# A fourth Strassen step per gate and up chunk, with part of the weight sums formed by accumulating transfers

## The chip, the cores and the metric

The kernel runs on one core of one Trainium2 chip. The metric is the device time of one execution in microseconds (us). Engines are named as in the profile: PE is TensorE's matmul, PEld its weight load, DVE is VectorE, ACT is ScalarE, POOL is GpSimd, SP is SyncE, which here only starts transfers.

## The reference

Two transformer blocks in float32 on 256 tokens of width 2048. The change touches only the gate and up products of the second block's feed-forward part (width 5632, that is 11 chunks of 512 columns):

```
h2 = rms_norm(x, g_ffn[i])
x = x + (jax.nn.silu(h2 @ w_gate[i]) * (h2 @ w_up[i])) @ w_down[i]
```

## The kernel before

**Products.** Every matrix product is done three times over: an operand is split into `hi` (rounded to the float32r type) and `lo` (what is left), and a product is hi x hi + lo x hi + hi x lo. The weights are what moves: they come from memory in items of 1 MB (128 partitions, 4 pieces or "quads" of 512 columns), ACT writes `whi` (a rounding copy, L1673), DVE writes `wlo` (raw minus whi, L2288), and PE consumes both. Every item is one unit of the order of work, and each engine takes the items in the same order. `whi` and `wlo` have three slots (SPLIT), so the conversion of item g can begin when PE has finished item g-3 (`mm_done`). The raw tile has a ring of four slots in this stage; SP starts the next load into a slot when DVE has finished with it.

**Pairs.** A chunk of gate and up takes the 16 blocks of 128 rows of h2 in 8 pairs. A pair of token tiles x a pair of row blocks times (gate, up) is a 2 x 2 by 2 x 2 block product. It is done either directly (kind D: 8 block products, 24 matmuls of 512 columns, one item) or by Strassen's scheme (kind S: 7 block products, 21 matmuls), and `GUD_PLAN` says which: before, "DDSDSDSD". A pair of kind S is two items. The first, B, uses three of the raw quads as they are (9 matmuls). The second, T, uses four sums of quads (12 matmuls), built from the same load: with u0, u1 the two up quads and g0, g1 the two gate quads, the sums are u0+u1, g1+u1, then the second plus u0, and that plus g0. DVE forms the first two in one instruction of 1024 columns (L2296), the third in L2299, the fourth in L2301; ACT rounds them in two halves (L1680), and DVE subtracts in two halves (L2305).

**Chunk end.** At the end of a chunk DVE folds the PSUM banks of the products (L2777, L2780, L2787, L2790), ACT applies silu (L2226), DVE multiplies (L3050); the hidden tile is transposed by PE (L1330) ahead of steps 4 and 6 of the next chunk and split by ACT and DVE (L1721, L2335). These instructions stand at fixed places between the conversions of the items, which ACT and DVE make two items ahead of PE's place in the chunk. Chunks come in blocks of 4, 4 and 3; behind each block the down projection runs with plain items (24 matmuls each, L857 to L862).

**First chunk.** In the first of the 11 chunks the last two pairs of h2's own tiles are still being built by ACT and DVE between the items (`gud_f`, `gud_hi`, `gud_lo`).

Of the kernel before, what the change touches and what calls it, by code (L numbers as in the profile page):

```python
# [25 lines left out]
F32 = mybir.dt.float32  # L26
# [7 lines left out]
P = 128  # L34
# [158 lines left out]

FF1_PLAN, FF2_PLAN, GUD_PLAN = "DDSDDSDD", "DDSDDSDD", "DDSDSDSD"
FF_BLOCKS, GUD_PAIRS = 4, (4, 4, 3)
# [50 lines left out]
ITEM_OF = [g for g in range(len(KINDS)) if KINDS[g] != "T"]  # L246
SLOTS = 5


# [54 lines left out]
def build(nc, a, out):  # L304
# [3 lines left out]
    with ctx:  # L308
# [73 lines left out]
        ff2_t = tiles("ff2", FF2_PLAN, W_AT, W_AT + tile_bytes(FF2_PLAN))  # L382
        gud_t = tiles("gud", GUD_PLAN, B_AT, W_AT + 16 * KB)
        E_AT = A_AT + 2 * tile_bytes(FF1_PLAN)
# [75 lines left out]
        def sem(name):  # L460
            return ctx.enter_context(nc.semaphore(name))
# [35 lines left out]
        fill_free, gate_b0 = sem("fill_free"), sem("gate_b0")  # L497
        mm_half, w_hi_half = sem("mm_half"), sem("w_hi_half")
        t_sum, t_hi, f_in, f_sum = sem("t_sum"), sem("t_hi"), sem("f_in"), sem("f_sum")
        bank_done, s1_out, q_free, silu_done, gud_hid = map(sem, (  # L500
# [144 lines left out]
        def v2(ap):  # L645

            return ap.rearrange("p (t n) -> p t n", t=2)
# [3 lines left out]
        def _(sp):  # L651
# [22 lines left out]
            def load_pair(src1, src2, c, step):  # L674

                n = w.n["group"]
                room(n)
                into = raw_of(n).rearrange("p (k f n) -> p k f n", k=2, f=2)
                for f, src in enumerate((src1, src2)):
                    sp.dma_start(into[:, :, f, :], src[:, 2 * step:2 * step + 2, c:c + COLS]  # L680
                                 ).then_inc(raw_in[SLOT[n]], 16)
                w.n["group"] += 1
# [108 lines left out]
        def _(pool):  # L791
            with nc.allow_non_contiguous_dma(reason="small rows"):
# [27 lines left out]
                for n, g in enumerate(("q_norm_2", "k_norm_2")):  # L820
                    pool.dma_start(qkg[:, n, :], a[g].rearrange("(a n) -> a n", a=1).to_broadcast([P, D2])
                                   ).then_inc(con2_in, 16)

                pool.wait_ge(w_lo, MARK["gud_end"])
                pool.wait_ge(mm_done, MARK["gud_end"])
# [829 lines left out]
        def _(act):  # L1655
# [19 lines left out]
            def sums_hi(g):  # L1675

                for n in range(2):
                    act.wait_ge(t_sum, 2 * SUMS_BEFORE[g] + 1 + n)
                    part = slice(2 * n * COLS, 2 * (n + 1) * COLS)
                    nc.scalar.activation(whi[:, g % SPLIT, part], tsum[:, g % SPLIT, part], ACT.Copy  # L1680
                                         ).then_inc(w_hi if n else t_hi, 1)

# [581 lines left out]
        def _(dve):  # L2264
# [26 lines left out]
            def weight_sums(g):  # L2291

                slot, r, n = g % SPLIT, raw_of(load_of(g)), SUMS_BEFORE[g]
                t = tsum[:, slot, :]
                dve.wait_ge(mm_done, g + 1 - SPLIT)
                V.tensor_tensor(v2(t[:, 0:2 * COLS]), both(r[:, col(3)]), v2(r[:, COLS:3 * COLS]), ALU.add  # L2296
                                ).then_inc(t_sum, 1)
                dve.wait_ge(t_sum, 2 * n + 1)
                link(V.tensor_tensor(t[:, col(2)], t[:, col(1)], r[:, col(1)], ALU.add))  # L2299
                linked()  # L2300
                V.tensor_tensor(t[:, col(3)], t[:, col(2)], r[:, col(0)], ALU.add).then_inc(t_sum, 1)  # L2301
                for k in range(2):
                    dve.wait_ge(w_hi if k else t_hi, g + 1 if k else n + 1)
                    part = slice(2 * k * COLS, 2 * (k + 1) * COLS)
                    last = V.tensor_tensor(wlo[:, slot, part], t[:, part], whi[:, slot, part].bitcast(F32),  # L2305
                                           ALU.subtract)
                last.then_inc(w_lo, 1)
# [843 lines left out]
```

## Time and profile before

| | |
|---|---|
| median of 3 runs | 2763.66 us (2761.6 to 2764.61) |
| profiled execution | 2762.97 us, its span 2761.2 us |
| PE busy | 2736.2 us, 99% |
| DVE busy | 1882.3 us, 68% |
| ACT busy | 1406.1 us, 51% |
| POOL busy | 14.8 us, 1% |
| DMA | 508.18 MB, mean 184 GB/s |

Shares over the whole span average stages of different kinds. The stage of the change runs from 1940 to 2589 us with the down projections in it, and what bounds it is read there. A row that gives an engine's idle time names what ended that idle time. The spans on POOL are those of issuing a transfer; how long the transfer itself took is given as the time from issue to landing.

### The profile page before, as it was taken

To read this page: it belongs to the slowest core of one execution; us is meant where nothing else is said; L and a number is where in the kernel's file an instruction comes from. 1 tells how busy PE (TensorE), PEld (TensorE's weight loads), DVE (VectorE), ACT (ScalarE), POOL (GpSimd) and SP (SyncE) were. 2 spreads that over 40 slices of the span, in tenths; PEclk is the share of its full clock that TensorE was granted. 3 is DMA by queue.
4 is the path that set the end of the run, shared out by engine and by line. 5 is a ranking of instruction groups with operands and counts; after the bars stand their busy time and mean duration, and the time that the engine had idled before them with its cause. 6 is when DMAs were issued, how large, how long until landed. Compare 5 with 4: busy or idle time off the path is not lost.

```text
span 2761.2 us, 30992 instructions
## 1 busy us (share of the span) xinstructions
PE 2736.2 (99%) x12990; PEld 2270.7 (82%) x12990; DVE 1882.3 (68%) x1699; ACT 1406.1 (51%) x1532; POOL 14.8 (1%) x28
## 2 busy tenths in 40 slices
PE   9999999999999999999999999999999999999999
PEld 7888778888888888888888888888788888888887
DVE  5445765455468878878788685665788488659765
ACT  5435663345556556465465544344554355435553
POOL 0000000000000000000000000000000000000000
PEclk9999999999999999999999999999999999999999
DMA  7745036555445555555555654545556555656555
GB/s 235 222 147 168 31 108 211 191 190 198 170 153 201 188 205 176 201 199 186 209 189 182 217 196 149 183 157 197 195 188 210 197 183 198 214 181 200 185 180 173
DMA packets 225082, 508.18 MB, mean 184 GB/s; under 512 B 9570, under 2 KB 20400, under 8 KB 224048
## 3 DMA queue, kind: packets, MB, share of 16 engines
q1 hardware_dynamic: 222752, 495.62, 53.6%
q0 software_dynamic: 2016, 10.36, 1.2%
q8 instruction: 103, 1.69, 0.2%
q14 instruction: 35, 0.29, 0.0%
q10 hardware_dynamic: 176, 0.23, 0.0%
HBM read 504.08 MB, written 2.10 MB: 183 GB/s over the span
## 4 chain that ended last, share of the span: by engine, by line
PE 79%; DVE 5%; ACT 2%; issue 1%; DMA 1%; ACTq 0%
PE acc L857 13%; PE acc L858 13%; PE acc L862 13%; PE acc L1340 6%; PE acc L1341 6%; PE acc L1345 6%; PE tb L1345 6%; PE tb L1340 6%; PE tb L1341 6%; DVE wlo L2288 2%; ACT whi L1673 1%; PE tb L842 1%; PE tb L1330 1%; DVE ff_lo L2757 1%; DVE tsum L2296 0%
## 5 line engine op out<-in xcount | busy, mean ns | idle before, releaser
L2288 DVE TENSOR_TENSOR wlo<-raw,whi 128x2048 fp32r<-128x2048 f32 (+2 forms) x465 | 1023.8, 2212 | 570.0 <-ACT whi L1673 569.3
L1673 ACT ACTIVATE whi<-raw 128x2048 fp32r<-128x2048 f32 (+2 forms) x465 | 858.0, 1853 | 593.1 <-PE acc L862 315.5
L857 PE MATMUL acc<-whi,ahi 128*128 128x512 f32 (+1 forms) x1456 | 566.6, 390 | 0.9 <-ACT z L1713 0.5
L858 PE MATMUL acc<-whi,alo 128*128 128x512 f32 (+1 forms) x1456 | 562.2, 387 | 0.0
L862 PE MATMUL acc<-wlo,ahi 128*128 128x512 f32 (+1 forms) x1456 | 357.6, 387 | 0.0
L857 PEld LDWEIGHTS acc<-whi,ahi 128*128 128x128 f32 x1456 | 273.9, 188 | 56.6 <-ACT z L1713 0.9
L858 PEld LDWEIGHTS acc<-whi,alo 128*128 128x128 f32 x1456 | 274.1, 188 | 54.4
L862 PEld LDWEIGHTS acc<-wlo,ahi 128*128 128x128 f32 x1456 | 271.0, 188 | 55.5
L1680 ACT ACTIVATE whi<-tsum 128x1024 fp32r<-128x1024 f32 x130 | 138.1, 1062 | 264.6 <-DVE tsum L2296 239.2
L1340 PE MATMUL acc<-whi,ff_hi 128*128 128x512 f32 x512 | 202.2, 395 | 7.2 <-DVE h L2360 3.9
L1341 PE MATMUL acc<-whi,ff_lo 128*128 128x512 f32 x512 | 199.8, 390 | 0.0
L1340 PE MATMUL tb<-whi,ff_hi 128*128 128x512 f32 x480 | 189.1, 394 | 0.0
L1341 PE MATMUL tb<-whi,ff_lo 128*128 128x512 f32 x480 | 187.3, 390 | 0.0
L1345 PE MATMUL acc<-wlo,ff_hi 128*128 128x512 f32 x512 | 163.2, 390 | 0.0
L2305 DVE TENSOR_TENSOR wlo<-tsum,whi 128x1024 fp32r<-128x1024 f32 x130 | 158.4, 1222 | 0.0
L1345 PE MATMUL tb<-wlo,ff_hi 128*128 128x512 f32 x480 | 156.2, 390 | 0.0
L1340 PE MATMUL acc<-whi,gud_hi 128*128 128x512 f32 x352 | 138.0, 392 | 3.2 <-ACT whi L1680 2.1
L1341 PE MATMUL acc<-whi,gud_lo 128*128 128x512 f32 x352 | 137.4, 390 | 0.0
L1340 PE MATMUL tb<-whi,gud_hi 128*128 128x512 f32 x319 | 125.8, 395 | 0.0
L1341 PE MATMUL tb<-whi,gud_lo 128*128 128x512 f32 x319 | 124.4, 390 | 0.0
L1340 PEld LDWEIGHTS acc<-whi,ff_hi 128*128 128x128 f32 x512 | 96.1, 188 | 29.3 <-DVE ff_lo L2757 4.4
L1345 PE MATMUL acc<-wlo,gud_hi 128*128 128x512 f32 x352 | 116.2, 391 | 0.0
(408 smaller groups left out, 3653.1 us busy)
## 6 DMA issues: line engine op xcount, KB each, us to landing
raw<-in_w_ff SPq DMA_DIRECT2D x128, 1024.0 KB, 5.0
raw<-in_w_in SPq DMA_DIRECT2D x119, 1024.0 KB, 5.1
raw<-in_w_gate SPq DMA_DIRECT2D x88, 512.0 KB, 3.9
raw<-in_w_up SPq DMA_DIRECT2D x88, 512.0 KB, 4.8
raw<-in_w_down SPq DMA_DIRECT2D x44, 1024.0 KB, 5.1
raw<-in_w_out SPq DMA_DIRECT2D x16, 1024.0 KB, 5.2
raw<-in_w_o SPq DMA_DIRECT2D x16, 1024.0 KB, 5.1
raw<-in_w_ple_gate SPq DMA_DIRECT2D x16, 1024.0 KB, 5.2
```

Source lines behind the costliest of these rows:

```text
L842: last = nc.tensor.transpose((into or tb[w.n["turn"] % 2])[:, n * P:(n + 1) * P], src, ident)
L857: nc.tensor.matmul(out_(t), hi[:, kt, tt(t)], whi[:, slot, wc(k)], start=first and k == 0, stop=False)
L858: nc.tensor.matmul(out_(t), lo[:, kt, tt(t)], whi[:, slot, wc(k)], start=False, stop=False)
L862: mm = nc.tensor.matmul(out_(t), hi[:, kt, tt(t)], wlo[:, slot, wc(k)], start=False, stop=last and k == len(kts) - 1)
L1330: last = nc.tensor.transpose(turn_bank[:, n * P:(n + 1) * P], src, ident)
L1340: nc.tensor.matmul(o, t.hi[:, tile, :], whi[:, slot, col(quad)], start=start, stop=False)
L1341: nc.tensor.matmul(o, t.lo[:, tile, :], whi[:, slot, col(quad)], start=False, stop=False)
L1345: return nc.tensor.matmul(o, t.hi[:, tile, :], wlo[:, slot, col(quad)], start=False, stop=stop)
L1673: nc.scalar.activation(whi[:, g % SPLIT, 0:n_], raw_of(n)[:, 0:n_], ACT.Copy).then_inc(w_hi, 1)
L1680: nc.scalar.activation(whi[:, g % SPLIT, part], tsum[:, g % SPLIT, part], ACT.Copy).then_inc(w_hi if n else t_hi, 1)
L2288: V.tensor_tensor(wlo[:, g % SPLIT, 0:n_], raw_of(load_of(g))[:, 0:n_], whi[:, g % SPLIT, 0:n_].bitcast(F32), ALU.subtract).then_inc(w_lo, 1)
L2305: last = V.tensor_tensor(wlo[:, slot, part], t[:, part], whi[:, slot, part].bitcast(F32), ALU.subtract)
```

## The change

`GUD_PLAN` becomes "DDSSDSSD": four pairs of kind S (steps 2, 3, 5, 6) and four of kind D. The first two of the four weight sums of every T item of this stage (u0+u1 and g1+u1) are no longer formed by DVE. POOL starts two plain transfers into a tile `tpre` (u0 and g1, 256 KB each), waits for both (`pre_in`), and starts two accumulating transfers that add u1 to each half (`pre_sum`). There are two such tiles, used in turn; the loads for the n-th sum wait until DVE has finished T item n-2 (`w_lo`). ACT rounds the first half and DVE subtracts it straight from `tpre`; DVE still forms the third and fourth sum. Since u1 as a raw quad is then used by nobody, SP leaves it out of the load of an S pair (768 KB instead of 1 MB). The feed-forward part of the first block has its own plans and keeps DVE's sums.

```diff
-FF1_PLAN, FF2_PLAN, GUD_PLAN = "DDSDDSDD", "DDSDDSDD", "DDSDSDSD"
+FF1_PLAN, FF2_PLAN, GUD_PLAN = "DDSDDSDD", "DDSDDSDD", "DDSSDSSD"
+SUM_ITEM = [g for g in range(len(KINDS)) if KINDS[g] == "T"]
+GUD_SUMS = SUMS_BEFORE[MARK["gud"]]
...
-        gud_t = tiles("gud", GUD_PLAN, B_AT, W_AT + 16 * KB)
+        gud_t = tiles("gud", GUD_PLAN, B_AT, W_AT + 12 * KB)
+        tpre = [sb("tpre0", [P, 2, COLS], F32, W_AT + 8 * KB), sb("tpre1", [P, 2, COLS], F32, B_AT + 27 * KB)]
...
                 for f, src in enumerate((src1, src2)):
-                    sp.dma_start(into[:, :, f, :], src[:, 2 * step:2 * step + 2, c:c + COLS]
+                    ks = 1 if f and GUD_PLAN[step] == "S" else 2
+                    sp.dma_start(into[:, 0:ks, f, :], src[:, 2 * step:2 * step + ks, c:c + COLS]
                                  ).then_inc(raw_in[SLOT[n]], 16)
...
+                pool.wait_ge(mm_done, MARK["gud"] - 3)
+                wg, wu, n = ktiles(a["w_gate_2"]), ktiles(a["w_up_2"]), 0
+                for b, pairs in enumerate(GUD_PAIRS):
+                    for c in range(pairs):
+                        for step in [k for k in range(len(GUD_PLAN)) if GUD_PLAN[k] == "S"]:
+                            at = slice((4 * b + c) * COLS, (4 * b + c + 1) * COLS)
+                            into = tpre[n % 2]
+                            if n >= 2:
+                                pool.wait_ge(w_lo, SUM_ITEM[GUD_SUMS + n - 2] + 1)
+                            pool.dma_start(into[:, 0, :], wu[:, 2 * step, at]).then_inc(pre_in, 16)
+                            pool.dma_start(into[:, 1, :], wg[:, 2 * step + 1, at]).then_inc(pre_in, 16)
+                            pool.wait_ge(pre_in, 32 * (n + 1))
+                            for k in range(2):
+                                pool.dma_start(into[:, k, :], wu[:, 2 * step + 1, at], accum_op=ALU.add
+                                               ).then_inc(pre_sum, 16)
+                            n += 1
...
+                m = SUMS_BEFORE[g] - GUD_SUMS
                 for n in range(2):
-                    act.wait_ge(t_sum, 2 * SUMS_BEFORE[g] + 1 + n)
                     part = slice(2 * n * COLS, 2 * (n + 1) * COLS)
-                    nc.scalar.activation(whi[:, g % SPLIT, part], tsum[:, g % SPLIT, part], ACT.Copy
-                                         ).then_inc(w_hi if n else t_hi, 1)
+                    src = tsum[:, g % SPLIT, part]
+                    if m >= 0 and n == 0:
+                        act.wait_ge(mm_done, g + 1 - SPLIT)
+                        act.wait_ge(pre_sum, 32 * (m + 1))
+                        src = tpre[m % 2][:, :, :].rearrange("p k n -> p (k n)")
+                    else:
+                        act.wait_ge(t_sum, 2 * SUMS_BEFORE[g] + 1 + n)
+                    nc.scalar.activation(whi[:, g % SPLIT, part], src, ACT.Copy).then_inc(w_hi if n else t_hi, 1)
...
+                m = n - GUD_SUMS
+                pre = t[:, 0:2 * COLS] if m < 0 else tpre[m % 2][:, :, :].rearrange("p k n -> p (k n)")
+                if m < 0:
...
+                else:
+                    dve.wait_ge(pre_sum, 32 * (m + 1))
+                    V.tensor_tensor(t[:, col(2)], pre[:, col(1)], r[:, col(1)], ALU.add).then_inc(t_sum, 1)
+                    dve.wait_ge(t_sum, 2 * n + 1)
                 V.tensor_tensor(t[:, col(3)], t[:, col(2)], r[:, col(0)], ALU.add).then_inc(t_sum, 1)
```

What the change does to the order of DVE's instructions, in the conversions of the items from the first B of a chunk on. In the names, `tsum` is the tile of sums, `tpre` the new tiles, numbers behind a name are those of the buffers. Before (one B and T, a D, the next B and T):

```order
L2288 TENSOR_TENSOR wlo<-raw_108,whi 128x1536 [waits w_hi]
L2296 TENSOR_TENSOR tsum<-raw_108 128x1024 [waits mm_done]
L2299 TENSOR_TENSOR tsum<-tsum,raw_108 128x512 [waits t_sum]
L2301 TENSOR_TENSOR tsum<-tsum,raw_108 128x512 [waits v_link]
L2305 TENSOR_TENSOR wlo<-tsum,whi 128x1024 [waits t_hi]
L2305 TENSOR_TENSOR wlo<-tsum,whi 128x1024 [waits w_hi]
L2288 TENSOR_TENSOR wlo<-raw_109,whi 128x2048 [waits w_hi]
L2288 TENSOR_TENSOR wlo<-raw,whi 128x1536 [waits w_hi]
L2296 TENSOR_TENSOR tsum<-raw 128x1024 [waits mm_done]
L2299 TENSOR_TENSOR tsum<-tsum,raw 128x512 [waits t_sum]
```

The same place now, where the lines have moved down in the file (L2288 is L2315, L2305 is L2338):

```order
L2315 TENSOR_TENSOR wlo<-raw_110,whi 128x1536 [waits w_hi]
L2332 TENSOR_TENSOR tsum<-tpre_103,raw_110 128x512 [waits pre_sum,mm_done]
L2334 TENSOR_TENSOR tsum<-tsum,raw_110 128x512 [waits t_sum]
L2338 TENSOR_TENSOR wlo<-tpre_103,whi 128x1024 [waits t_hi]
L2338 TENSOR_TENSOR wlo<-tsum,whi 128x1024 [waits w_hi]
L2315 TENSOR_TENSOR wlo<-raw_111,whi 128x1536 [waits w_hi]
L2332 TENSOR_TENSOR tsum<-tpre_104,raw_111 128x512 [waits pre_sum,mm_done]
L2334 TENSOR_TENSOR tsum<-tsum,raw_111 128x512 [waits t_sum]
L2338 TENSOR_TENSOR wlo<-tpre_104,whi 128x1024 [waits t_hi]
L2338 TENSOR_TENSOR wlo<-tsum,whi 128x1024 [waits w_hi]
L2315 TENSOR_TENSOR wlo<-raw,whi 128x2048 [waits w_hi]
L2315 TENSOR_TENSOR wlo<-raw,whi 128x1536 [waits w_hi]
```

The instruction of 1024 columns that began each T item is gone, its first instruction now waits for `pre_sum` as well, and two S pairs follow each other without a D item between them.

POOL's queue in this stage, where it had nothing before. L838 and L839 are the plain transfers, L842 the accumulating ones:

```order
L838 DMA tpre_103<-in_w_up 128x512 [waits w_lo]
L839 DMA tpre_103<-in_w_gate 128x512
L842 DMA tpre_103<-in_w_up 128x512 [waits pre_in]
L842 DMA tpre_103<-in_w_up 128x512
L838 DMA tpre_104<-in_w_up 128x512 [waits w_lo]
L839 DMA tpre_104<-in_w_gate 128x512
L842 DMA tpre_104<-in_w_up 128x512 [waits pre_in]
L842 DMA tpre_104<-in_w_up 128x512
```

POOL carries two waits per sum, one for the tile to be free and one for its own loads; the loads of one sum stand behind the accumulating transfers of the sum before it in the same queue.

## Rows read from the trace of the kernel before

**Rows 1.** The page's part 1, busy time.
```profile
PE 2736.2 (99%) x12990; PEld 2270.7 (82%) x12990; DVE 1882.3 (68%) x1699; ACT 1406.1 (51%) x1532; POOL 14.8 (1%) x28
```

**Rows 2.** Critical chain through the stage: start us, us, what.
```profile
1938.95 1.81 PE acc L862 x8
...
2051.54 0.91 PE tb L1345 x4
2093.99 0.91 PE tb L1345 x4
```

**Rows 3.** Windows: the first chunk, a later chunk, a PE gap, the stretch after it.
```profile
core 0: us, PE busy (x) PEld busy (x) DVE busy (x) ACT busy (x) POOL busy (x), PEclk, DMA share, GB/s
1940.00:1985.00 45.00, 41.76 (x179) 33.43 (x178) 33.93 (x34) 25.56 (x27) 0.00 (x0) 0.96 0.47 147
2009.09:2051.54 42.45, 42.45 (x192) 35.12 (x192) 37.88 (x32) 23.00 (x20) 0.00 (x0) 1.00 0.61 199
1976.70:1978.85 2.15, 0.04 (x2) 0.00 (x1) 2.12 (x4) 1.76 (x3) 0.00 (x0) 1.00 0.11 9
1980.40:1983.40 3.00, 3.00 (x9) 2.32 (x8) 2.77 (x2) 2.00 (x2) 0.00 (x0) 0.50 0.61 232
```

**Rows 4.** What PE waited for from 1935 to 2000 us: total, times, longest.
```profile
PE acc L1340 <- ACT whi L1680: 2.1, 1, 2.1
PE acc L1340 <- ACT whi L1673: 1.1, 1, 1.1
```

**Rows 5.** Groups in the later chunk, by shape: busy us, mean ns, idle before.
```profile
L2288 DVE TENSOR_TENSOR wlo<-raw,whi 128x2048 fp32r<-128x2048 f32 x5 | 11.4, 2289 | 3.8 <-ACT whi L1673 3.8
L2305 DVE TENSOR_TENSOR wlo<-tsum,whi 128x1024 fp32r<-128x1024 f32 x7 | 8.5, 1222 | 0.0
L2288 DVE TENSOR_TENSOR wlo<-raw,whi 128x1536 fp32r<-128x1536 f32 x3 | 5.3, 1753 | 0.0
L2296 DVE TENSOR_TENSOR tsum<-raw 128x1024 f32<-128x1024 f32 x3 | 3.7, 1219 | 0.0
L2301 DVE TENSOR_TENSOR tsum<-tsum,raw 128x512 f32<-128x512 f32 x3 | 2.1, 692 | 0.1
L1680 ACT ACTIVATE whi<-tsum 128x1024 fp32r<-128x1024 f32 x7 | 7.4, 1063 | 12.4 <-DVE tsum L2296 10.8 <-DVE tsum L2301 1.6
```

**Rows 6.** DVE's timeline in the first chunk, ahead of PE's 2.1 us wait.
```profile
1975.04 1.22 DVE L2296 TENSOR_TENSOR tsum<-raw 128x1024 f32<-128x1024 f32 x1
...
1977.01 0.69 DVE L2301 TENSOR_TENSOR tsum<-tsum,raw 128x512 f32<-128x512 f32 x1
```

**Rows 7.** A later chunk: PE's first matmul, DVE's end of its first T item.
```profile
2073.66 0.39 PE L1340 MATMUL acc<-whi,gud_hi 128*128 128x512 f32 x1
2082.69 2.43 DVE L2305 TENSOR_TENSOR wlo<-tsum,whi 128x1024 fp32r<-128x1024 f32 x2
```

**Rows 8.** Transfers in the later chunk; columns of part 2 in 40 slices.
```profile
GB/s 83 313 409 197 2 0 29 179 405 351 50 195 403 355 8 0 27 172 401 405 388 332 230 120 345 401 158 0 0 8 58 311 409 210 0 0 68 309 409 203
raw<-in_w_up SPq DMA_DIRECT2D x9, 512.0 KB, 4.8
raw<-in_w_gate SPq DMA_DIRECT2D x8, 512.0 KB, 3.9
```

**Rows 9.** Transfers of POOL's queue: KB each, us from issue to landing.
```profile
gfin<-in_g_final POOLq DMA_DIRECT2D x1, 1024.0 KB, 5.2
bple<-in_b_ple_gate POOLq DMA_DIRECT2D x1, 1024.0 KB, 4.9
pin<-in_p POOLq DMA_DIRECT2D x1, 256.0 KB, 6.0
grows<-in_g_ffn POOLq DMA_DIRECT2D x1, 8.0 KB, 2.8
```

**Rows 10.** POOL's timeline at the end of the stage, the issues of two of these.
```profile
2588.52 0.54 POOL L826 DMA_DIRECT2D bple<-in_b_ple_gate  x1 [1047.85 <-PE tb L1345]
2589.05 0.71 POOL L828 DMA_DIRECT2D pin<-in_p  x1
```

More of the change, by code:

```diff
@@ L498, in build @@
         mm_half, w_hi_half = sem("mm_half"), sem("w_hi_half")
+        pre_in, pre_sum = sem("pre_in"), sem("pre_sum")
         t_sum, t_hi, f_in, f_sum = sem("t_sum"), sem("t_hi"), sem("f_in"), sem("f_sum")
@@ L2295, in weight_sums @@
                 dve.wait_ge(mm_done, g + 1 - SPLIT)
[L2296 to L2300, printed above, removed]
+                m = n - GUD_SUMS
+                pre = t[:, 0:2 * COLS] if m < 0 else tpre[m % 2][:, :, :].rearrange("p k n -> p (k n)")
+                if m < 0:
+                    V.tensor_tensor(v2(pre), both(r[:, col(3)]), v2(r[:, COLS:3 * COLS]), ALU.add).then_inc(t_sum, 1)
+                    dve.wait_ge(t_sum, 2 * n + 1)
+                    link(V.tensor_tensor(t[:, col(2)], pre[:, col(1)], r[:, col(1)], ALU.add))
+                    linked()
+                else:
+                    dve.wait_ge(pre_sum, 32 * (m + 1))
+                    V.tensor_tensor(t[:, col(2)], pre[:, col(1)], r[:, col(1)], ALU.add).then_inc(t_sum, 1)
+                    dve.wait_ge(t_sum, 2 * n + 1)
                 V.tensor_tensor(t[:, col(3)], t[:, col(2)], r[:, col(0)], ALU.add).then_inc(t_sum, 1)
@@ L2304, in weight_sums @@
                     part = slice(2 * k * COLS, 2 * (k + 1) * COLS)
-                    last = V.tensor_tensor(wlo[:, slot, part], t[:, part], whi[:, slot, part].bitcast(F32),
-                                           ALU.subtract)
+                    last = V.tensor_tensor(wlo[:, slot, part], t[:, part] if k else pre,
+                                           whi[:, slot, part].bitcast(F32), ALU.subtract)
                 last.then_inc(w_lo, 1)
```

## The prediction

> **What bounds the kernel now.** I read the page's first part, then the chain through the stage, then windows inside it, the groups of one chunk, the waits, and last the transfers. PE is busy 99% of the span [rows 1], so only fewer or faster matmuls make the kernel faster, unless a new wait appears. In the stage of the change the chain is PE's: eight matmuls of 512 columns take 1.81 us, 0.227 us each, and a chunk follows the other in 42.45 us [rows 2]. Three S pairs (21 matmuls each) and five D pairs (24 each) are 183 matmuls, 41.5 us; the two sets of transposes take the other 0.97 us. In that chunk PE has no idle time at all, while DVE works 37.9 of the 42.45 us and ACT 23.0 [rows 3]. So DVE is the engine that is near: its 89% can't be raised by much.
>
> **PE.** A fourth S pair in place of a D pair takes 3 matmuls out of each chunk: 3 x 0.227 = 0.68 us, in 11 chunks 7.5 us. That is all that the change can give in the steady chunks.
>
> **DVE.** Per T item the add of 1024 columns (1.22 us) goes, and one of 512 (0.69 us) now reads the finished sum; the rest is unchanged: 0.69 + 0.69 + 2 x 1.22 = 3.8 us instead of 5.0 [rows 5]. Per chunk: three T items save 3.7 us; the D pair that becomes an S pair gives up 2.3 us and takes 1.75 + 3.8 [rows 5]. The balance is -3.7 + 3.3 = -0.4 us, so about 37.5 of 41.8 us. ACT gets the B and T copies (1.5 + 2 x 1.06 us [rows 5]) for one of 1.9 us, with 18 us free. Neither becomes the bound by its sum. What matters is the order: the pairs of kind S now touch. I lay the chunk out from PE's first matmul, with 5.44 us per D, 2.04 per B, 2.72 per T item and 0.49 ahead of steps 4 and 6. PE's items then end at 5.4, 10.9, 12.9, 15.6, 17.7, 20.4, 26.3, 28.4, 31.1, 33.6, 36.3 and 41.8 us. An item's conversion starts when PE is done with the third item before it. The last B may start at 26.3: ACT 1.5, DVE 1.75, so DVE turns to the last T at 29.6, adds twice until 31.0, ACT's second half is done at 32.1, and PE wants it at 33.6: it is hidden by 1.5 us. DVE's subtractions end at 33.5, the split of the transposed tile at 34.1, and the last D's `wlo` (ACT's copy from 32.7 to 34.6, then 2.3 us) at 36.9, where PE asks for it after two matmuls at 36.8. That is a wait of 0.1 to 0.2 us that is new; I take 0.17 in the 8 chunks that have such transposes, 1.4 us. If DVE were faster nothing more would come, if it were slower by some tenths each would be paid 11 times.
>
> **The accumulating transfers** are the part whose price the trace does not show. The path that decides is the last sum of a chunk. Its tile and that of the sum before it come free when DVE ends T items 2 and 1. Before, DVE ends the first T 11.5 us after PE's first matmul (2085.1 against 2073.7 [rows 7]); with 1.22 us less work, and the rest of the schedule as above, 10.7 is what I take. From there POOL has until 29.6 us, when DVE turns to the last T: 18.9 us. In them it must, one behind the other, load sum 3's tile, accumulate into it, load sum 4's tile (behind those accumulations in the same queue), and accumulate into that. POOL's second wait, for its own loads, is what makes this serial; behind the waiting instruction stand the next sum's loads, and ACT and DVE both wait for `pre_sum` in front of all later conversions, so PE is next. With F for the fixed part of a transfer from issue to landing, L for moving a pair of loads (512 KB) and A for a pair of accumulations, the path is 3F + 2L + 2A (one F is shared, since the loads of sum 4 follow sum 3's accumulations in the queue).
> F: POOL's 1 MB transfers land 4.9 and 5.2 us after issue [rows 9]; at the 409 GB/s that the slices of the later chunk reach [rows 8] the moving is 2.6 us of it, so 2.3 to 2.6 us are fixed; 8 KB take 2.8. I take 2.5. SP's pairs agree: the second of two 512 KB loads, issued some 0.4 us behind the first, lands after 4.8 [rows 8].
> L: alone 0.52 MB at 409 GB/s is 1.3 us. The high end is the transfer of 256 KB that was issued at 2589.05 and landed 6.0 us later, 1.6 us behind the one issued at 2588.52 that took 4.9 [rows 9, 10]: twice that is 3.3 us. SP's loads run in bursts with free slices between them [rows 8], so I take 1.8, nearer to the low end.
> A: the low end is a plain load alone, 1.3 us. An accumulation has to read its destination as well as its source; the high end is twice the slow row, 6.6 us. I take 3.3, the slow row itself, because that is the nearest POOL transfer beside SP's.
> Path: 7.5 + 3.6 + 6.6 = 17.7 us, hidden by 1.2 us. At the low ends it is 6.9 + 2.6 + 2.6 = 12.1, hidden by 7; at the high ends 8.4 + 6.6 + 13.2 = 28.2, late by 9.3 in every chunk. The point from which it binds is L + A = 5.7 us. The other three sums of a chunk have more room, since a D or the chunk's turn lies before them.
> The Trainium skill ("Collectives: The Full Stack", Part 3, the section on the bandwidth ceiling) has a rule that speaks against the change: a reducing transfer has two source reads and so moves at half the rate of a copy. By it A would be 2.6 us alone and about 3.6 beside SP's loads, and the path 16.3 to 18.3 us: still hidden, but by little. No row of this trace shows an accumulation, so the rule is neither borne out nor refuted here.
>
> **The transfers as a whole.** A chunk moved 8 x 1.05 = 8.4 MB at a DMA share of 0.61 [rows 3]. Now SP moves 7.3 MB, POOL 2.1 MB plain and 2.1 MB accumulating. Plain bytes alone are a share of about 0.70; the accumulations add 0.15 if they cost as much as plain ones and 0.31 at twice that. There is room, but little at the upper price, and SP's loads, issued some 10 us ahead, would be the first to use it up.
>
> **The first chunk.** There DVE is late: PE is idle 3.24 of 45.0 us [rows 3], 2.1 and 1.1 us of it waiting for ACT's copies [rows 4]. The larger wait hangs on a T item, whose sums run from 1975.04 to 1977.7, then ACT's copy [rows 6]. Behind that gap the granted clock is 0.50 for 3.0 us [rows 3], that is 1.2 instead of 2.4 GHz; in these 3.0 us PE does the work of 1.5, so the gap costs 1.5 us more. With 1.2 us less in every T item, and T items one D earlier, the two waits shrink: I put the remainder at 1.2 us and the gap too short for the clock to fall, which would give 3.5 us, and take 2.5, between a full recovery (4.7) and a loss of 1.5 if the S pair that comes earlier lands on the building of the tiles.
>
> **The sum.** -7.5 + 1.4 - 2.5 = -8.6 us. From the profiled execution's 2762.97 us that is 2754.4; the median of the runs is 0.7 us above that execution, so 2755.
>
> **Rivals.**
> (B) The accumulating transfers take the place of DVE as the bound. At F 2.5, L 2.5 and A 4.4 the path is 21.3 us, late by 2.4 in each chunk. A chunk then takes 42.45 - 0.56 + 2.4 = 44.3, 11 of them cost 20 us, less 2.5 in the first: 2781. From a gap of about 2.1 us on, as in the first chunk, the clock can fall behind it, 1.5 us more each: 2797. For it: POOL's transfers of 256 KB land late beside SP's, and the path is serial. Against it: the bursts of rows 8 leave free slices, and the chain is short of binding by the prices taken.
> (C) Accumulations are far slower than copies (the high ends): late by 9.3 us, with the clock 10.2 net per chunk, 11 x 10.2 less 2.5: 2873. For it nothing but the absence of a row; against it that a copy's price would have to rise fivefold.
> (D) The sums are in time, but the denser order or the crowded transfers cost some tenths per item (SP's loads late, DVE's last D later than 0.17 us), or the first chunk gives nothing: 0.5 us more per chunk, 2760.
>
> **How the numbers follow.** The forecast (A) has 0.45, B 0.28, C 0.12, D 0.15. What a measurement of this kernel can tell from no change is about 0.2%, 5.5 us: below 2758.1 is faster, above 2769.2 slower. Faster: 0.38 of A, 0.04 of B (a lateness of some tenths), 0.02 of D: 0.44. Same: 0.07 of A, 0.04 of B, 0.09 of D: 0.20. Slower: 0.20 of B, 0.12 of C, 0.04 of D: 0.36. The forecast's own range is 2750 to 2760. The range for 8 in 10 goes up through B with the clock to 2803 and leaves C out.
>
> **What would show it.** Right: PE items of the stage without idle, a chunk period of 41.8 to 42.0 us, 33 matmuls fewer; POOL's accumulations landing within some 6 us of their issue; the first chunk's PE gaps under 1.5 us and the clock at 1.00. Wrong: PE or ACT waiting for a DMA into `tpre` in the last S pair of each chunk (B: 1 to 4 us, with a clock of 0.5 behind the longer ones; C: about 10 us), or ACT waiting for raw loads there (D). The forecast falls if L + A is above 5.7 us.

## The result and the profile after

The changed kernel takes 2807.59 us (median of 4 runs, 2803.14 to 2810.25) against 2764.14 us before, on the same chip: a ratio of 1.0156, 95% interval 1.0144 to 1.0168. It is slower by 43 us; the forecast was 9 us faster, and the time lies 4.6 us above the upper end of the range. The profiled execution took 2803.14 us, its span is 2801.3 us.

The page's part 1, which answers to [rows 1]:

```profile
PE 2744.8 (98%) x12957; PEld 2271.2 (81%) x12957; DVE 1877.5 (67%) x1713; ACT 1421.6 (51%) x1554; POOL 142.2 (5%) x204
```

The 33 matmuls are gone, yet PE is busy 8.6 us longer: some of the others ran at the lower clock. What PE waited for from 1935 to 2640 us (total, times, longest):

```profile
PE acc L1361 <- ACT whi L1708: 28.7, 12, 3.8
PE acc L1366 <- DVE wlo L2315: 4.1, 4, 1.1
PE acc L1361 <- ACT whi L1694: 1.8, 1, 1.8
```

L1708 is ACT's copy of a T item. Before, PE had 3.2 us of waits in the stage, all in the first chunk [rows 4]; now it has 34.6. That is 31.4 us more, and with 8.6 us more of busy time it makes the 40.1 us between the two spans to 0.1. Counted from one chunk's first fold on DVE to the next's inside a block, a chunk follows the other in 45.6 to 47.9 us (before 42.45, and 42.8 to 43.0 for the second chunk of a block).

The critical chain through one steady chunk (start us, us, what) says where the wait comes from:

```profile
2050.87 2.37 DVE wlo L2338 x2
2053.23 0.29 issue
2053.52 0.56 POOL tpre L838
2054.08 5.88 DMA tpre<-in_w_gate
2059.96 0.49 issue
2060.45 0.56 POOL tpre L842
2061.01 7.34 DMA tpre<-in_w_up
2068.44 0.70 DVE tsum L2332
2069.16 0.70 DVE tsum L2334
2069.89 1.07 ACT whi L1708
2071.00 0.49 PE acc L1361
2071.49 0.23 PE acc L1362
2071.73 0.23 PE tb L1361
2071.96 0.37 PE tb L1362
2072.33 0.43 PE acc L1361
```

DVE ends a T item and frees its tile at 2053.2, the last sum's two loads follow, then its accumulations, and 15.2 us later DVE can begin the last T item of the chunk. Before, the chain in the later chunks was PE's [rows 2]. DVE's timeline shows how long it stood there, and PE's what it cost (in brackets the idle time before, and what ended it):

```profile
2063.23 1.76 DVE L2315 TENSOR_TENSOR wlo<-raw,whi 128x1536 fp32r<-128x1536 f32 x1 [1.19 <-ACT whi L1694]
2068.44 0.69 DVE L2332 TENSOR_TENSOR tsum<-tpre,raw 128x512 f32<-128x512 f32 x1 [3.45 <-DMA tpre<-in_w_up]
```

```profile
2071.00 0.49 PE L1361 MATMUL acc<-whi,gud_hi 128*128 128x512 f32 x1 [2.10 <-ACT whi L1708]
```

The sum is late by 3.45 us for DVE; 1.3 us of it is hidden by the slack that the prediction counted (1.5 us), and PE stands for 2.1. Behind the gap some eight matmuls start 0.43 instead of 0.23 us apart, 1.6 us more in all. Windows (columns as in [rows 3]) of the two transfers of the path, of that slow stretch, and of a whole chunk:

```profile
2054.08:2060.45 6.37, 6.37 (x32) 5.26 (x31) 6.33 (x6) 3.45 (x4) 0.56 (x3) 1.00 1.04 346
2061.57:2068.35 6.78, 6.78 (x34) 5.60 (x33) 2.23 (x2) 1.49 (x1) 1.80 (x3) 1.00 1.01 274
2071.00:2075.30 4.30, 4.30 (x12) 3.40 (x13) 3.84 (x3) 4.03 (x3) 1.81 (x3) 0.60 1.00 237
2009.09:2055.00 45.91, 42.21 (x189) 34.25 (x188) 37.13 (x33) 24.31 (x21) 11.58 (x16) 1.00 0.87 252
```

Over a chunk the DMA engines are busy 0.87 of the time. In just the two stretches that the path passes through they are full (1.04 and 1.01; a share is the time of the packets that start in the window, so it can pass 1), and the second of them moves only 274 GB/s, against the 409 of plain loads [rows 8]. From issue to landing (KB each, median us) POOL's transfers take, from 1990 to 2600 us:

```profile
tpre<-in_w_up POOLq DMA_DIRECT2D x111, 256.0 KB, 6.6
tpre<-in_w_gate POOLq DMA_DIRECT2D x37, 256.0 KB, 5.7
```

SP fills the engines there. Its timeline over the same stretch:

```profile
2050.90 0.37 SPq L685 DMA_DIRECT2D raw<-in_w_gate  x1
2051.31 0.54 SPq L685 DMA_DIRECT2D raw<-in_w_up  x1
2056.12 0.37 SPq L685 DMA_DIRECT2D raw<-in_w_gate  x1
2056.53 0.47 SPq L685 DMA_DIRECT2D raw<-in_w_up  x1
2059.71 0.37 SPq L685 DMA_DIRECT2D raw<-in_w_gate  x1
2060.12 0.47 SPq L685 DMA_DIRECT2D raw<-in_w_up  x1
```

Three item loads start within 9 us. This is not chance: an item that DVE finishes frees a raw slot for SP and, if it is a T item, 2.4 us later a tile for POOL (DVE's fourth sum ends at 2050.87, its last subtraction at 2053.2).

### The profile page after: what moved, and what is told of

Same layout as the page of the kernel before. It is cut to its first block, busy times and chain, and to the rows that moved or that the text cites. A ratio compares the mean times of both kernels' runs of the same rounds, so it can differ in the third digit from the quotient of the medians.

```text
span 2801.3 us, 31226 instructions
## 1 busy us (share of the span) xinstructions
PE 2744.8 (98%) x12957; PEld 2271.2 (81%) x12957; DVE 1877.5 (67%) x1713; ACT 1421.6 (51%) x1554; POOL 142.2 (5%) x204
## 4 chain that ended last, share of the span: by engine, by line
PE 71%; DVE 7%; DMA 5%; ACT 4%; issue 2%; POOL 0%; ACTq 0%; DVEq 0%
PE acc L878 13%; PE acc L879 13%; PE acc L883 13%; PE acc L1361 5%; PE acc L1366 5%; PE acc L1362 5%; PE tb L1361 5%; PE tb L1362 5%; PE tb L1366 5%; DMA tpre<-in_w_up 3%; DVE wlo L2315 3%; ACT whi L1694 2%; DMA tpre<-in_w_gate 2%; DVE wlo L2338 1%; PE tb L863 1%
## 5 line engine op out<-in xcount | busy, mean ns | idle before, releaser
L2315 DVE TENSOR_TENSOR wlo<-raw,whi 128x2048 fp32r<-128x2048 f32 (+2 forms) x465 | 1018.8, 2200 | 577.1 <-ACT whi L1694 576.1
L1708 ACT ACTIVATE whi<-tsum 128x1024 fp32r<-128x1024 f32 x108 | 114.7, 1062 | 179.9 <-DVE tsum L2326 118.6
L2338 DVE TENSOR_TENSOR wlo<-tsum,whi 128x1024 fp32r<-128x1024 f32 x108 | 131.8, 1223 | 0.0
L1366 PE MATMUL acc<-wlo,gud_hi 128*128 128x512 f32 x352 | 122.0, 397 | 4.1 <-DVE wlo L2315 4.1
```

Of the source, the lines that this page charges most:

```text
L1366: return nc.tensor.matmul(o, t.hi[:, tile, :], wlo[:, slot, col(quad)], start=False, stop=stop)
L1708: nc.scalar.activation(whi[:, g % SPLIT, part], src, ACT.Copy).then_inc(w_hi if n else t_hi, 1)
L2315: V.tensor_tensor(wlo[:, g % SPLIT, 0:n_], raw_of(load_of(g))[:, 0:n_], whi[:, g % SPLIT, 0:n_].bitcast(F32), ALU.subtract).then_inc(w_lo, 1)
L2338: last = V.tensor_tensor(wlo[:, slot, part], t[:, part] if k else pre, whi[:, slot, part].bitcast(F32), ALU.subtract)
```

## The experiments

The theory (S) after reading this: two tiles make the last sum's load wait for the T item two before it, and load plus accumulation, beside SP's bursts, take longer than is left. Rivals: the denser order makes DVE late by itself (O); the bytes and accumulations load the DMA engines so that everything is late (T); the issues on POOL are the price (I). The expectations below call T "theory B"; it is not the prediction's rival B, which is S. Times before in these runs were 2764.06 to 2764.38 us.

**The plan alone.** The new plan, all sums formed by DVE, no transfers of POOL.

```diff
-GUD_SUMS = SUMS_BEFORE[MARK["gud"]]
+GUD_SUMS = 10 ** 6
...
-                    ks = 1 if f and GUD_PLAN[step] == "S" else 2
+                    ks = 2
...
-                pool.wait_ge(mm_done, MARK["gud"] - 3)
                 wg, wu, n = ktiles(a["w_gate_2"]), ktiles(a["w_up_2"]), 0
-                for b, pairs in enumerate(GUD_PAIRS):
+                for b, pairs in enumerate(()):
```

> One part of the change alone: the plan DDSSDSSD, with all four sums formed by DVE as before and u1 loaded by SP; POOL starts nothing. Theory S (the change is slow because the load-then-accumulate path of POOL is late for the last sums of a chunk, each late sum stopping PE): without transfers no wait on them, but DVE now has 42.4 us of work per chunk of 41.8, so DVE itself is late by some tenths to 2 us per chunk: 2762 to 2785 us. Theory O (the order with two S pairs side by side is what costs): as slow as the change or slower, 2800 us or more, with PE waiting for ACT's copy of the sums in the second pair of each group. Theory B (the DMA engines are full, raw loads are late): as S, since the bytes are those of before.

Measured: 2791.49 us, ratio 1.0099 [1.0084, 1.0114], 6.5 us above the range of theory S. A chunk takes 44.8 us; DVE works 42.1 of them and waits only for ACT's copies in between, so DVE sets the pace. What PE waited for in the stage, its two largest:

```profile
PE acc L1360 <- ACT whi L1707: 15.2, 23, 3.0
PE acc L1365 <- DVE wlo L2314: 11.1, 11, 1.2
```

So the fourth S pair needs the relief of DVE, and the changed kernel pays more for the relief than the plan costs without it.

**The transfers alone.** The old plan, its three sums per chunk formed by transfers.

```diff
-FF1_PLAN, FF2_PLAN, GUD_PLAN = "DDSDDSDD", "DDSDDSDD", "DDSSDSSD"
+FF1_PLAN, FF2_PLAN, GUD_PLAN = "DDSDDSDD", "DDSDDSDD", "DDSDSDSD"
```

> The other part alone: the plan of before (DDSDSDSD, three sums per chunk) with the first two sums formed by accumulating transfers. Theory S: the three sums stand a D pair apart and every tile is free 20 us or more ahead, so all are in time; PE's matmuls are those of before: 2761 to 2766 us. Theory B: 10.5 MB per chunk instead of 8.4 keep the DMA engines above 80%, raw loads or sums come late, 2770 us or more. Theory O: as before, 2764.

Measured: 2760.84 us, ratio 0.9987 [0.9977, 0.9996], chunks of 42.45 us as before, at a DMA share of 0.84 and 251 GB/s. That is nearly the share of the changed kernel (0.87), and nothing is late in steady chunks. A high mean share is not the cause by itself. Nearly all of the 3.5 us comes from the first chunk, which is 3.1 us shorter than before: PE waits 1.5 us there instead of 3.2, and the granted clock stays at 1.00. That is the relief of DVE which the prediction had counted on, still in the old order.

**A copy for the accumulation.** The same transfers, plain: the sum isn't formed.

```diff
-                                pool.dma_start(into[:, k, :], wu[:, 2 * step + 1, at], accum_op=ALU.add
+                                pool.dma_start(into[:, k, :], wu[:, 2 * step + 1, at]
```

> The changed kernel with the two accumulating transfers of each sum replaced by plain ones of the same size to the same place (so the sums hold u1 alone and the output is not the reference's). All waits and issues stay. Theory S with a dear accumulation (A is well above a copy's time): the second phase gets shorter by 1.5 to 3 us per sum, twice in the path, 2765 to 2785 us. If an accumulation costs what a copy costs and only the two serial phases matter: 2800 to 2808, no change. Theory B (full engines): between these, as far as the DMA share falls.

Measured: 2773.54 us, ratio 1.0032 [1.0021, 1.0043]. A transfer of the second pair lands 4.3 us after its issue instead of 6.9 (medians), an issue takes 0.54 instead of 0.90 us, and the gate load ahead of it lands after 4.6 us instead of 5.7. 34 of the 47 us above the free-running variants go; even with copies 13 remain.

**Nobody waits for the sums.** POOL forms the first two sums of the stage only, and all later T items use what is in the tiles.

```diff
                             if n >= 2:
+                                break
...
-                        act.wait_ge(pre_sum, 32 * (m + 1))
+                        act.wait_ge(pre_sum, 32 * min(m + 1, 2))
...
-                    dve.wait_ge(pre_sum, 32 * (m + 1))
+                    dve.wait_ge(pre_sum, 32 * min(m + 1, 2))
```

> The changed kernel with transfers into the two tiles for the first two sums only; all later sums use what lies there (so the output is not the reference's), nobody waits for POOL any more, and SP still leaves u1 out. It prices everything but the transfers. Theories S and B: the gain I forecast for the hidden case, 2753 to 2758 us, with chunk periods of 41.8 to 42.0 us. Theory O: 2775 us or more.

Measured: 2760.87 us, ratio 0.9989 [0.9979, 0.9998]. This is what the new order gives once the sums cost nothing: chunks of 42.08 us, 47 us less than the changed kernel, and still only 3.5 us less than before. So O is wrong as a cause of the loss, but the forecast of 2755 was out of reach even with sums for nothing.

**Three tiles.** A third tile (in two halves of 2 KB per partition), so that a sum's loads wait for the T item three before it; same transfers and same bytes, nothing is left out.

```diff
+        tpre2 = [sb("tpre2a", [P, COLS], F32, B_AT + 30 * KB), sb("tpre2b", [P, COLS], F32, W_AT + 38 * KB)]
+        pre_half = lambda m, k: tpre2[k][:, :] if m % 3 == 2 else tpre[m % 3][:, k, :]
...
-                            if n >= 2:
-                                pool.wait_ge(w_lo, SUM_ITEM[GUD_SUMS + n - 2] + 1)
-                            pool.dma_start(into[:, 0, :], wu[:, 2 * step, at]).then_inc(pre_in, 16)
+                            if n >= 3:
+                                pool.wait_ge(w_lo, SUM_ITEM[GUD_SUMS + n - 3] + 1)
+                            pool.dma_start(pre_half(n, 0), wu[:, 2 * step, at]).then_inc(pre_in, 16)
...
```

> The changed kernel with a third tile for the sums that are formed ahead, so that the loads of sum n wait for T item n-3 instead of n-2; bytes, accumulations and POOL's two-phase order stay (one tile in three is in two parts, which costs ACT 0.1 and DVE 0.2 us there). Theory S (each late sum is the two-phase path measured from the freeing of a tile): POOL then needs only 4 x (6.3 us for the loads + 1.8 for issuing the accumulations + some tenths) = 34 us per chunk of 42, the sums are in time and PE's waits on them go: 2761 to 2768 us. Theory B (the 16 DMA engines have no time left: a share of 0.87 over chunks of 45.8 us is 39.9 us, 0.95 of a chunk of 42): transfers get slower as the chunk gets shorter, and half or more of the loss stays: 2780 to 2805 us.

Measured: 2760.49 us, ratio 0.9987 [0.9977, 0.9997]. All 47 us are back. What PE waited for in the stage, and a window over a steady chunk:

```profile
PE acc L1364 <- ACT whi L1697: 1.8, 1, 1.8
PE acc L1364 <- ACT whi L1714: 1.8, 1, 1.8
```

```profile
2009.00:2051.00 42.00, 41.99 (x190) 34.37 (x189) 37.17 (x33) 24.45 (x23) 11.49 (x17) 1.00 0.90 271
```

The transfers are no faster (accumulations land after 6.5 us, loads after 6.3 to 6.8), the DMA share is higher (0.90), and PE has no idle time in the chunk. T is wrong: the same amount at a higher share costs nothing once the last sum may start earlier. Span by span it is 42.2 us: 31.0 of waits in the stage and 12.1 of PE's busy time (2732.7 against 2744.8), less 0.9 us by which PE's idle time outside the stage differs.

**The S pairs apart.** Two tiles, with D items between the first three S pairs.

```diff
-FF1_PLAN, FF2_PLAN, GUD_PLAN = "DDSDDSDD", "DDSDDSDD", "DDSSDSSD"
+FF1_PLAN, FF2_PLAN, GUD_PLAN = "DDSDDSDD", "DDSDDSDD", "DSDSDSSD"
```

> The changed kernel with the plan DSDSDSSD: the same four S pairs, 33 matmuls fewer, two tiles, the same transfers, but only one pair of S pairs side by side. Theory S: fewer T items have their tile freed less than 20 us ahead, and the sums arrive more evenly: 2765 to 2785 us. Theory B: the bytes are the same in the same time, so 2795 us or more. Should the first D item alone ahead of an S pair collide with DVE's folds at the chunk's start, PE waits for ACT's copy there, and the gain is lost with POOL in time.

Measured: 2786.7 us, ratio 1.0082 [1.0067, 1.0097]; waits for `whi` of T items 14.6 us in 11, for `wlo` of D items 8.8 in 9. 21 of the 47 us go, somewhat less than theory S had set (at most 2785). One pair of neighbours is left in the chunk, and its second sum still has too little time.

**One phase, plain.** Only the two loads, no accumulation: the tiles hold u0 and g1. POOL starts the loads of a sum when those of the sum before have landed.

```diff
+                            if n:
+                                pool.wait_ge(pre_in, 32 * n)
...
-                            pool.wait_ge(pre_in, 32 * (n + 1))
-                            for k in range(2):
-                                pool.dma_start(into[:, k, :], wu[:, 2 * step + 1, at], accum_op=ALU.add
-                                               ).then_inc(pre_sum, 16)
...
-                        act.wait_ge(pre_sum, 32 * (m + 1))
+                        act.wait_ge(pre_in, 32 * (m + 1))
...
-                    dve.wait_ge(pre_sum, 32 * (m + 1))
+                    dve.wait_ge(pre_in, 32 * (m + 1))
```

> The changed kernel with the accumulating transfers left out: ACT and DVE take the tiles as the two plain loads leave them (so the output is not the reference's). Each sum has one phase of some 5 us from the freeing of its tile, and 9.4 MB per chunk move. Theories S and B alike: in time, 2760 to 2763 us, as in the run with two sums only (2760.9). If it is slower than 2766, SP's raw loads are held up already by plain traffic.

Measured: 2761.51 us, ratio 0.9991 [0.9982, 1.0]; the loads land after 3.0 us.

**One phase, accumulating.** Only the two accumulations, onto what is in the tile (it is loaded once).

```diff
-                            pool.dma_start(into[:, 0, :], wu[:, 2 * step, at]).then_inc(pre_in, 16)
-                            pool.dma_start(into[:, 1, :], wg[:, 2 * step + 1, at]).then_inc(pre_in, 16)
-                            pool.wait_ge(pre_in, 32 * (n + 1))
+                                pool.wait_ge(pre_sum, 32 * n)
+                            if n < 2:
+                                for k, w_ in enumerate((wu[:, 2 * step, at], wg[:, 2 * step + 1, at])):
+                                    pool.dma_start(into[:, k, :], w_).then_inc(pre_in, 16)
+                            pool.wait_ge(pre_in, 32 * min(n + 1, 2))
```

> The changed kernel with only the accumulating transfers (after the first two sums no plain loads go ahead of them, so the tiles keep adding u1 and the output is not the reference's); POOL starts those of a sum when those of the sum before have landed. One phase again, now the dear one, of 6 to 8 us. Theory S: the last sum of a chunk has 11.6 us from the freeing of its tile, so it is in time: 2760 to 2765 us. If an accumulation hurts by what it takes from the DMA engines and not by its place in a two-phase path (theory B), a good part of the 47 us stays: 2775 us or more.

Measured: 2760.73 us, ratio 0.9988 [0.9978, 0.9997]; the accumulations land after 5.3 us. Together with the experiment in which nobody waits for the sums, these two price an accumulated byte. The same window in each, first without transfers of POOL, then with 2.1 MB plain, then with 2.1 MB accumulating:

```profile
2009.00:2051.00 42.00, 41.99 (x190) 34.41 (x189) 37.16 (x33) 24.41 (x22) 0.00 (x0) 1.00 0.56 176
```

```profile
2009.00:2051.00 42.00, 41.99 (x190) 34.41 (x189) 37.16 (x32) 24.39 (x22) 4.27 (x8) 1.00 0.69 226
```

```profile
2009.00:2051.00 42.00, 41.99 (x189) 34.44 (x188) 37.16 (x33) 24.41 (x22) 6.98 (x8) 1.00 0.85 226
```

The plain transfers add 0.13 to the DMA share, the accumulating ones 0.29 at the same 226 GB/s: 2.2 times the engine time for the same bytes. (The page's part 3 gives the same over the whole execution: POOL's queue has 1.5% of the engines' time with 12.46 MB, 3.8% with 33.44 MB and 6.8% with 34.49 MB, so 5.3% for 22.0 MB accumulated against 2.3% for 21.0 MB plain.) The Trainium skill ("Collectives: The Full Stack", Part 3, the section on the bandwidth ceiling) says of the ring collectives that the reduce, with two source reads, moves at half the rate of the copy; these rows, from another kind of transfer, agree to about a tenth. DVE's own work stays at 37.2 us in all three windows, so POOL's issues do not slow its instructions. Either phase alone is hidden in every steady chunk; with two tiles only the two in series are late.

**Lighter loads of SP.** The changed kernel with SP's loads of D items cut to half their columns from the second chunk on (the rest of the tile stays as it was).

```diff
-                    sp.dma_start(into[:, 0:ks, f, :], src[:, 2 * step:2 * step + ks, c:c + COLS]
+                    nc_ = COLS if GUD_PLAN[step] == "S" or w.n["group"] < ITEM_OF.index(MARK["gud"]) + 8 else COLS // 2
+                    sp.dma_start(into[:, 0:ks, f, 0:nc_], src[:, 2 * step:2 * step + ks, c:c + nc_]
```

> The changed kernel with SP's loads for D pairs cut to half their columns (the other halves keep old data, so the output is not the reference's), beginning with the second chunk; POOL's transfers, tiles and waits stay. SP moves 5.2 MB per chunk instead of 7.3. In the changed kernel the path from the second T item to the last sum is 15.2 us (6.4 for the loads, 7.9 for the accumulations, the rest issue and semaphores) where 11.6 are free. If the transfers are long because they run beside SP's loads (what I mis-sized in L and A), it shrinks by 2 to 4 us and with it the wait and the slow clock behind it: 2762 to 2780 us. If the accumulation is slow by itself, the second phase stays near 7.9 us and the time above 2790 us.

Measured: 2781.71 us, ratio 1.0064 [1.005, 1.0078]. POOL's loads land after 4.3 and 4.6 us, the accumulations after 6.2. The time lies 2 us above the range set for long transfers beside SP's loads and 8 below the other. What stands beside POOL's transfers carries 26 of the 47 us.

**Three tiles, other orders.** "DSDSSDSD" and "DSSDSSDD"; the second:

```diff
-FF1_PLAN, FF2_PLAN, GUD_PLAN = "DDSDDSDD", "DDSDDSDD", "DDSSDSSD"
+FF1_PLAN, FF2_PLAN, GUD_PLAN = "DDSDDSDD", "DDSDDSDD", "DSSDSSDD"
```

> Three tiles, plan DSDSSDSD: the same four S pairs, but the last one stands alone, so that DVE's work on the last D item is not pushed behind two T items. The layout of the chunk by durations gives 41.8 us instead of 42.1 (no wait on the last D's wlo): 0.3 us in 11 chunks, 3 us: 2756 to 2759 us against 2760.5 of the three tiles with DDSSDSSD. If the first S pair, now right behind the first D, meets DVE's folds, up to 2765.

> Three tiles, plan DSSDSSDD: two D pairs at the end. By the same layout 41.8 us per chunk, and in the first chunk the last pair built is a D and a D, whose tiles need fewer instructions of DVE where it is late: 2754 to 2758 us. If POOL's sums for the first two S pairs come late because they stand right behind the chunk's turn, 2765 or more.

Measured: 2759.1 us, ratio 0.998 [0.9971, 0.9989], and 2756.7 us, ratio 0.9975 [0.9965, 0.9985]. The second is the fastest version, 7.4 us below before. Two D items stand at its end, so the split of the transposed tile no longer delays the last D's `wlo`: chunks take 41.77 us, 0.68 less than before. Its PE waits, all in the first chunk:

```profile
PE acc L1364 <- ACT whi L1714: 3.8, 3, 1.6
PE tb L1364 <- ACT whi L1697: 0.3, 1, 0.3
```

**One accumulating transfer for two.** The two of a sum become one of 512 KB that reads its source twice.

```diff
-                            for k in range(2):
-                                pool.dma_start(into[:, k, :], wu[:, 2 * step + 1, at], accum_op=ALU.add
-                                               ).then_inc(pre_sum, 16)
+                            pool.dma_start(into[:, :, :], wu[:, 2 * step + 1, at].unsqueeze(1).to_broadcast([P, 2, COLS]),
+                                           accum_op=ALU.add).then_inc(pre_sum, 16)
...
-                        act.wait_ge(pre_sum, 32 * (m + 1))
+                        act.wait_ge(pre_sum, 16 * (m + 1))
...
-                    dve.wait_ge(pre_sum, 32 * (m + 1))
+                    dve.wait_ge(pre_sum, 16 * (m + 1))
```

> The two accumulating transfers of a sum (256 KB each, same source) become one of 512 KB that reads the source twice; everything else as in the changed kernel, and the result is the same. It takes one issue (0.90 us) out of each sum but moves the same bytes. If the price of the accumulations is one of issue and fixed parts, the last sum of a chunk lands about 0.9 us earlier (late by 2.6 instead of 3.5 us), PE's gap in a chunk falls from 2.1 to 1.2 us, the clock stays up behind it, and the time is 2807.6 - 11 x (0.9 + 1.6) = 2780 us. If it is one of moving (engines reading source and destination), the transfer lands as late as the second of the two did, 6.9 us behind its issue or more, and the time is 2800 to 2810 us.

Measured: 2808.2 us, ratio 1.0162 [1.0145, 1.0179], no change against the 2807.6 of the changed kernel. The chain in the same chunk:

```profile
2054.84 5.96 DMA tpre<-in_w_gate
2060.79 0.48 issue
2061.28 7.60 DMA tpre<-in_w_up
```

From the end of the wait to the landing it is 8.1 us with one transfer and 8.4 with two (0.49 + 0.56 + 7.34), so half of the issue of 0.56 us that went is made up by the transfer. Over the last sums of the ten later chunks the medians from the first load's issue to the last landing are 15.2 us in both. I is wrong: the price is that of moving on engines that are full.

## Why the prediction was wrong

**PE's gain** (-7.5 us) was right. 33 matmuls went, and where nothing is in the way a chunk takes 42.45 - 0.68 = 41.77 us, as with three tiles and the plan DSSDSSDD.

**The wait on the last D's `wlo`** was forecast as 0.17 us in 8 chunks. Where the sums are in time (three tiles) the chunk is 42.08 us, so 0.31 us are lost, in every steady chunk, about 3 us instead of 1.4.

**The first chunk** was forecast at -2.5 us beside its three matmuls, 3.2 us shorter. From PE's first matmul of the stage to the start of the second D item of the next chunk it was 53.58 us before (1940.61 to 1994.19), and it is 53.80 in the changed kernel (1940.66 to 1994.46), the same 53.8 with three tiles and where nobody waits for POOL: 0.2 us longer. With the transfers alone, in the old order, it is 50.50 us (1943.02 to 1993.52), 3.1 shorter: the gain was there, and the new order took it away. The 2.1 us that PE waited for a T item [rows 4] became 0.7 in all. But the S pair that comes earlier put ACT's copy of the D item behind it late, while ACT was still building h2's tiles. The changed kernel's PE timeline:

```profile
1962.47 0.39 PE L1366 MATMUL tb<-wlo,gud_hi 128*128 128x512 f32 x1
1964.67 0.47 PE L1361 MATMUL acc<-whi,gud_hi 128*128 128x512 f32 x1 [1.81 <-ACT whi L1694]
```

```profile
1964.67:1972.00 7.33, 7.33 (x25) 5.93 (x26) 5.94 (x8) 3.76 (x5) 1.77 (x2) 0.77 0.67 198
```

PE stood for 1.81 us in a place without a wait before, and the granted clock of the 7.3 us behind it is 0.77. This is the "S pair that lands on the building of the tiles", which the prediction had as the loss at the end of the term's range. Where nobody waits for POOL the clock stays at 1.00 and PE waits 4.7 us in all instead of 3.1, with the same 53.8 in the end: I read from it that ACT and DVE set the length here, so that a slow PE only uses up its next wait.

**The path of the accumulating transfers** is the step that failed, and it carries the 47 us. The prediction put it as "17.7 us, hidden by 1.2 us", with L + A = 5.1 us and the chain binding from 5.7; measured it is 9.3. Its mechanism was right: POOL's two phases in series, with the next T item waiting behind them in ACT and DVE. Two things were not, and the first decides the sign.

The first is the prices. F + L was 4.3 us and took 6.4 (0.56 + 5.88); F + A was 5.8 and took 7.9 (0.56 + 7.34). With F at 2.5 that is L = 3.9 and A = 5.4 us, L + A = 9.3. L lies above even its high end of 3.3, A inside its range of 1.3 to 6.6; the values taken were 1.8 and 3.3. The accumulation's own price was not the mistake: by the DMA share it is 2.2 plain transfers, by my estimate some 2.9 us at the 1.3 us of a plain load, below the 3.3 taken. What was missed is the state of the engines at that place. From SP's bursts in [rows 8] the prediction concluded that there were free slices; but the bursts are started by the same ends of DVE's items that free the tiles, and POOL's 512 KB and its accumulations fall into them. Copies instead of accumulations give back 34 us, lighter loads of SP 26. Each takes time off the same 16 engines, so the two can't be added (they are more than the 47).

The second is the segment. The prediction added up both last sums from the first T's end (18.9 us available). The tile of the last sum comes free only when DVE ends the second T, 18.0 us after PE's first matmul; there POOL stood 2.07 us waiting for the tile, not for its queue. From there only 11.6 us are left, for one load and one accumulation: 10.1 us by the prices taken, 15.2 measured with the waits between them. Late by 3.5 us. With the prices taken this segment too would have been hidden, by 1.5 us, so it is the mis-sized L and A that turned a gain into a loss; the segment explains why it is late by 3.5 us, and why a third tile, which changes no transfer, brings back everything.

**The rivals.** B with the clock (2797) is what happened: PE waits 2.0 to 3.8 us in the last S pair of each of the ten later chunks, with the clock down behind seven of these waits. It was 11 us short. In the profiled execution the ten later chunks cost 39.9 us more than before, 4.0 each where B had 1.85 + 1.5, which makes 6.4; the first chunk cost 0.2, 0.6 less than B had it. The other 4.5 us are the distance from the profiled execution to the median of the runs, which had been 0.7 before. B had a slow clock in all eleven chunks; the trace has it in eight, the first among them. C's about 10 us did not come, nor D's wait for raw loads in place of B; D's smaller terms, the first chunk and the last D's `wlo`, did.

**Order and relief.** The plan alone costs 27 us, since DVE (42.1 us of work in a chunk, some 5 more than in the changed kernel) becomes the bound; the transfers alone give 3.5 (2760.84), 3.1 of them in the first chunk. Only both, with a third tile and the two D items at the end, give 7.4.

What stays open: that the building of h2's tiles makes ACT late in the first chunk was read from timelines, and no run took it out. Nor was it tried to start POOL's transfers at a moment away from SP's. Why the clock fell behind some waits and not behind others is open too.

## What to carry to other kernels

When a step moves from an engine to transfers, find the release that starts them and the wait that ends them for each buffer, and sum the phases in series between the two, for the last buffer too, not for the queue as a whole. Price them with what the DMA engines do in just that stretch: if the event that frees the buffer also starts another queue's loads, they can meet in every round, whatever the mean share says. Where such a path is late, try more depth first: here one tile of 4 KB per partition gave back 47 us, cheaper transfers 34, lighter neighbours 26, one issue less nothing.

## What the runs showed of the hardware

- An accumulating transfer in float32 from memory into a tile costs 2.2 times the DMA engine time of a plain one (0.29 against 0.13 of the share for the same 2.1 MB), and each of two started together, 256 KB each, lands 5.3 against 3.0 us after its issue (medians). One accumulating transfer for both is no faster than two: 15.2 us for the last sum of a chunk in both.
- Issues on POOL took 0.54 to 0.57 us plain and 0.86 to 0.90 us accumulating in the shortest and the median, 1.2 us for the merged one.
- The clock does not follow a gap's length alone. With nobody waiting for POOL gaps of 1.80 and 1.75 us in the first chunk left it at 1.00; with three tiles there were gaps of 1.77 and 1.76 us, and the clock fell behind the second; a gap of 3.09 us in the changed kernel (before 2117.78) was followed by matmuls of 0.23 us. So "from about 2.1 us on", as the prediction took it from one gap, is no rule. The first chunk in these two, first with nobody waiting:

```profile
1940.00:1985.00 45.00, 40.14 (x176) 31.31 (x174) 32.58 (x35) 25.89 (x29) 1.78 (x2) 1.00 0.54 174
```

```profile
1940.00:1985.00 45.00, 41.35 (x176) 32.65 (x174) 32.64 (x35) 25.49 (x29) 14.36 (x20) 0.96 0.91 259
```
